# Sums of squares halved on VectorE, paired compression matmuls, weight splits moved to GpSimd at four joints, and first loads in halves

## The reference, cut to what matters

```python
def first_block(x, ...):
    h = x
    for layer in range(2):
        if layer == 1:
            shared = nsa_shared_kv(h, kv_norm, kv_w, ...)   # k and v of three branches; one is compressed by an MLP
        normed = rms_norm(h, mix_norm_pre[layer])
        mixed = retention_mixer(normed, ...) if layer == 0 else nsa_mixer(normed, ..., shared)
        h = h + rms_norm(mixed, mix_norm_post[layer])
        normed = rms_norm(h, ffn_norm_pre[layer])
        h = h + rms_norm(swiglu_ffn(normed, ...), ffn_norm_post[layer])
    return h

def second_block(x, ...):
    h = modulate(rmsnorm(x, norm1_g), sh1, sc1)
    u_a, v_a, q, k, v, gates = split(h @ w_in)              # k and v also for a context of 256 tokens
    merged = g_a * (chunk_gmlp(u_a, v_a) @ w_proj_a) + g_b * (window_gqa(q, k, v, ...) @ w_proj_b)
    x = x + g1 * (merged @ w_out)
    h2 = modulate(rmsnorm(x, norm2_g), sh2, sc2)
    return rmsnorm(x + g2 * expert_choice_ffn(h2, ...), final_g)   # 16 experts, 32 tokens each
```

## Time and profile before

| | |
|---|---|
| median of three runs | 2094.96 us (2092.45 to 2096.02) |
| time of the profiled execution | 2095.24 us |
| span of its trace | 2093.4 us |
| mean granted TensorE clock | 0.903 |
| busy: TensorE, VectorE, ScalarE, GpSimd | 1661.2, 709.5, 579.1, 113.8 us |
| read from HBM | 594.71 MB |

### The profile page before, as it was taken

The page is one execution under the profiler, slowest core; times in us unless marked ns, Lnnn a source line. Parts: engine busy times, 40 slices in busy tenths (PEclk is TensorE's granted clock), DMA queues, the critical chain, the costliest instruction groups (busy, mean ns, idle before and its releaser), DMA issues.

```text
span 2093.4 us, 27147 instructions
## 1 busy us (share of the span) xinstructions
PE 1661.2 (79%) x11764; PEld 1155.0 (55%) x11764; DVE 709.5 (34%) x1020; ACT 579.1 (28%) x959; POOL 113.8 (5%) x127
## 2 busy tenths in 40 slices
PE   7999999999889999999996765565556565555665
PEld 7899999998469999897796311111111111111111
DVE  5456655563656755657655100000000000000001
ACT  4455444443665344436652100000000000000000
POOL 1001000000310300002300000000000000000000
PEclk9999999999999999999998978878887878888777
DMA  9545685557694655263265799999999999999995
GB/s 305 185 141 178 120 247 185 186 172 217 246 316 149 207 185 183 81 202 103 100 262 201 304 427 430 426 429 427 428 428 427 429 426 429 427 428 428 429 427 214
DMA packets 156380, 603.54 MB, mean 288 GB/s; under 512 B 6550, under 2 KB 109127, under 8 KB 128471
## 3 DMA queue, kind: packets, MB, share of 16 engines
q1 hardware_dynamic: 147712, 587.23, 71.8%
q10 hardware_dynamic: 7704, 11.23, 1.8%
q0 software_dynamic: 864, 3.61, 1.5%
HBM read 594.71 MB, written 4.19 MB: 286 GB/s over the span
## 4 chain that ended last, share of the span: by engine, by line
PE 52%; DMA 41%; DVE 4%; ACT 2%; issue 1%; POOL 0%; DVEq 0%; ACTq 0%
PE ps L663 19%; DMA dense_tables<-in_w_exp_gate 13%; DMA dense_tables<-in_w_exp_up 13%; DMA dense_tables<-in_w_exp_down 13%; PE ps L732 11%; PE ps L717 3%; PE ps L1230 2%; PE ps L1089 2%; PE ps L685 2%; PE ps L640 1%; DVE split_operands L572 1%; PE ps L1251 1%; PE ps L1122 1%; PE ps L1112 1%; PE ps L897 1%
## 5 line engine op out<-in xcount | busy, mean ns | idle before, releaser
L572 DVE TENSOR_TENSOR split_operands<-dense_ring,split_operands 128x1024 fp32r<-128x1024 f32 x288 | 349.9, 1257 | 272.7 <-ACT split_operands L564 272.4
L663 PE MATMUL ps<-split_operands 128*128 128x256 f32 x3456 | 426.0, 284 | 15.9 <-DVE split_operands L572 13.2
L663 PEld LDWEIGHTS ps<-split_operands 128*128 128x128 f32 x3456 | 419.7, 193 | 17.4 <-issue 14.0
L564 ACT ACTIVATE split_operands<-dense_ring 128x1024 fp32r<-128x1024 f32 x288 | 288.6, 1050 | 324.4 <-PE ps L663 159.5
L2226 DVE TENSOR_TENSOR arena<-arena,ps 128x512 f32<-128x512 f32 x16 | 11.0, 688 | 861.2 <-PE ps L1230 861.2
L1230 PE MATMUL ps<-dense_ring,arena 128*32 128x512 f32 x624 | 99.8, 771 | 80.1 <-DMA dense_ring<-in_w_exp_gate 41.4
L1230 PE MATMUL ps<-late_expert_slots,arena 128*32 128x512 f32 x592 | 105.0, 845 | 71.8 <-DMA late_expert_slots<-in_w_exp_up 36.0
L732 PE MATMUL ps<-split_operands 128*128 128x256 f32 x1248 | 151.6, 283 | 2.4 <-DVE split_operands L582 2.1
L732 PEld LDWEIGHTS ps<-split_operands 128*128 128x128 f32 x1248 | 150.2, 192 | 4.4 <-DVE split_operands L582 2.5
L1230 PE MATMUL ps<-arena 128*32 128x512 f32 x624 | 93.6, 726 | 59.7 <-DMA arena<-in_w_exp_gate 33.9
L732 PE MATMUL ps<-hidden_split,split_operands 128*128 128x256 f32 x960 | 118.6, 283 | 0.8 <-DVE split_operands L572 0.8
(11 more groups left out here) (297 smaller groups left out, 1739.8 us busy)
## 6 DMA issues: line engine op xcount, KB each, us to landing
dense_ring<-in_ffn_w_in SPq DMA_DIRECT2D x44, 1024.0 KB, 5.1
arena<-in_w_exp_gate SPq DMA_DIRECT2D x20, 2048.0 KB, 46.8
dense_ring<-in_w_exp_up SPq DMA_DIRECT2D x20, 2048.0 KB, 46.5
late_expert_slots<-in_w_exp_down SPq DMA_DIRECT2D x20, 2048.0 KB, 46.7
dense_ring<-in_w_exp_gate SPq DMA_DIRECT2D x19, 2048.0 KB, 46.2
arena<-in_w_exp_up SPq DMA_DIRECT2D x19, 2048.0 KB, 45.9
late_expert_slots<-in_w_exp_up SPq DMA_DIRECT2D x19, 2048.0 KB, 45.6
arena<-in_w_exp_down SPq DMA_DIRECT2D x19, 2048.0 KB, 45.5
```

What stands on the lines that cost most here:

```text
L564: act.activation(w_hi[:, n % 2, c], ring[U % RING][:, c], ACT.Copy).then_inc(hi_ready, 1)
L572: dve.tensor_tensor(w_lo[:, n % 2, c], ring[U % RING][:, c], w_hi[:, n % 2, c], ALU.subtract).then_inc(lo_ready, 1)
L663: mm = pe.matmul(ps[:, bank, b * T:b * T + T], left, right, start=k == 0 and i == 0, stop=k == 7 and i == 2)
```

## The change

What it does, by parts:

- **Squares.** `add_squares` on VectorE adds chunks of squares before TensorE sums them. The four norms ahead of a block (`N_PRE0`, `N_PREF0`, `N_PRE1`, `N_PREF1`) then need 2 ones matmuls instead of 8, the four in the joints 4, and retention's heads 2 instead of 4. In `pair_products` the norm now stands behind all products.
- **Joints.** ScalarE runs a tiny Sqrt before the squares, and `roots` before the split of U+1. VectorE no longer splits U+1: GpSimd does.
- **Compression.** k and v are multiplied in turn, in columns 0 to 59 and 64 to 123 of the array; the four weight units are loaded in that order.
- **K and V.** `U_K` and `U_V` leave `WHOLE`: the tokens' keys and values come from split units. The context's stay unsplit.
- **Start.** x is passed in with 4 KB rows by half, and x and the first unit are loaded in halves, in turn; splits and products of the first unit go by halves.

```diff
-WHOLE = set(range(U_W1, U_NQ)) | set(range(U_ADA, U_NO)) | {U_IN2 + 4, U_IN2 + 5}
+WHOLE = set(range(U_W1, U_NQ)) | set(range(U_ADA, U_NO))
+ADDED = {N_PRE0: (0,), N_POST0: (0, 3), N_PREF0: (0,), N_POSTF0: (0, 3), N_PRE1: (0,), N_POST1: (0, 3),
+         N_PREF1: (0,), N_POSTF1: (0, 3)}
 # SyncE
-            sp.dma_start(h[:], a["xT"].rearrange("(k p) t -> p k t", p=P)).then_inc(x_in, 16)
+            for half in range(2):
+                k = slice(4 * half, 4 * half + 4)
+                sp.dma_start(h[:, k, :], a["x_rows"].rearrange("p (k t) -> p k t", k=DC)[:, k, :]).then_inc(x_in[half], 16)
+                sp.dma_start(slot8(U_RET)[:, k, :], first[:, k, :]).then_inc((half_landed, landed[0])[half], 16)
 # TensorE
-                for q in range(4):
-                    pe.wait_ge(sq_ready, 4 * n + q + 1)
+                for q in ADDED.get(n, range(4)):
+                    if n in ADDED and q == 0:
+                        pe.wait_ge(sq_added, 2 * n + 2)
+                    else:
+                        pe.wait_ge(sq_ready, 4 * n + q + 1)
                     for c in (2 * q, 2 * q + 1):
...
                 mm.then_inc(used, 1)
-                between()
                 for k in range(4, 8):
                     mm = chunk(1, k)
                 mm.then_inc(used, 1)
+                norm(n)
...
-                pe.wait_ge(osq, hd + 1)
-                for e in range(4):
-                    mm = pe.matmul(ps[:, 4, 0:T], ones[:], sq[:, e, :], start=e == 0, stop=e == 3)
+                pe.wait_ge(osq_added, hd + 1)
+                for e in range(2):
+                    mm = pe.matmul(ps[:, 4, 0:T], ones[:], sq[:, e, :], start=e == 0, stop=e == 1)
...
+                    for w in range(2):
+                        for kind in range(2):
+                            take(U_W1 + 2 * w + kind)
+                        for c in range(8):
+                            for kind in range(2):
+                                mm = pe.matmul(ps[64 * kind:64 * kind + 60, kind, 0:T], blocks[:, kind, 8 * w + c, :],
+                                               slot8(U_W1 + 2 * w + kind)[:, c, :], start=w == 0 and c == 0,
+                                               stop=w == 1 and c == 7)
...
-            keys(xn, 7).then_inc(used, 1)
-            values(xn, 4).then_inc(used, 1)
+            col_T(U_K, 7)
+            col_tok(U_V, 4)
 # ScalarE, post()
                 split_hi(act, U)
+                act.activation(table_of[:], ones[:, 0:1], ACT.Sqrt)
...
+                roots(n)
                 split_hi(act, U + 1)
-                roots(n)
 # ScalarE, compression
+                rows = slice(64 * kind, 64 * kind + 60)
+                taken(act, U_W1 + 2 + kind)
+                act.activation(cmp_hid[rows, 0:T], ps[rows, kind, 0:T], ACT.Silu).then_inc(c_act, 1)
                 split_hi(act, U_NQ + kind)
 # VectorE
+            def add_squares(n):
+                steps = ((4, 4, 4), (2, 2, 4)) if len(ADDED[n]) == 1 else ((2, 2, 2), (2, 4, 3))
+                for i, (chunks, other, squared) in enumerate(steps):
+                    dve.wait_ge(sq_ready, 4 * n + squared)
+                    if i:
+                        dve.wait_ge(sq_added, 2 * n + i)
+                    dve.tensor_tensor(sq[:, 0:chunks, :], sq[:, 0:chunks, :], sq[:, other:other + chunks, :],
+                                      ALU.add).then_inc(sq_added, 1)
...
                 split_lo(dve, U)
-                split_lo(dve, U + 1)
+                add_squares(n)
                 inverse(n)
...
+                add_squares(n)
+                dve.wait_ge(lo_ready, 2 * SPLIT_NO[gate_unit(f, 0) + 1] + 2)
                 split_lo(dve, gate_unit(f, 1))
                 inverse(n)
...
-            for U in (U_IN2 + 2, U_IN2 + 3, U_UA):
+            dve.wait_ge(lo_ready, 2 * SPLIT_NO[U_IN2 + 1] + 2)
+            for U in (U_IN2 + 2, U_IN2 + 3, U_K, U_V):
                 split_lo(dve, U)
 # GpSimd, each in its place in the queue
+            split_lo(pool, U_F0 + 1)
             pool.wait_ge(brow_ev, 1)
             pool.dma_start(bias_dram, ...)
+            split_lo(pool, U_KV + 1)
...
+            split_lo(pool, U_F1 + 1)
             pool.wait_ge(gains_set, 1)
...
+            split_lo(pool, U_IN2 + 1)
```

More of the change, by code:

```diff
@@ L473, in load_expert @@
                 sp.dma_start(dst, src).then_inc(e_landed[g % ERING], 16)
-            for u in range(24):
+            for u in range(1, 24):
                 if 8 <= u < 16:
@@ L673, in col_tok, with pair_products @@
                 col_products(U, bank, lambda b, w, x: (x[:, b * P:b * P + P], w), 0, x0)
-            def pair_products(U, banks, place, x0, between):
+            def pair_products(U, banks, place, x0, n):
                 def chunk(v, k):
@@ L756, in _ @@
             pe.wait_ge(ones_set, 1)
-            for u in range(2):
-                col_products(U_RET + u, 5 + 2 * u, lambda b, w, x: (w[:, b::2], x), x0=X_RET if u == 0 else None)
-                if u == 0:
-                    norm(N_PRE0)
+            hi, lo = parts_of(U_RET)
+            for k in range(8):
+                if k % 4 == 0:
+                    pe.wait_ge(lo_ready, k // 4 + 1)
+                pe.wait_ge(xlo_ready, k + 1)
+                for b in range(2):
+                    for i, (w, x) in enumerate(((hi, x_hi), (hi, x_lo), (lo, x_hi))):
+                        mm = pe.matmul(ps[:, 5, b * T:b * T + T], w[:, k, b::2], x[:, k, :],
+                                       start=k == 0 and i == 0 and b == 0, stop=k == 7 and i == 2,
+                                       skip_group_check=True)
+            mm.then_inc(used, 1)
+            norm(N_PRE0)
+            col_products(U_RET + 1, 7, lambda b, w, x: (w[:, b::2], x))
             pe.wait_ge(first_in, FIRST_IN)
@@ L874, in _ @@
             bias_table(1)
-            pair_products(U_KV, (1, 3), by_feature, X_KV, lambda: norm(N_PRE1))
+            pair_products(U_KV, (1, 3), by_feature, X_KV, N_PRE1)
             for u in range(2, 6):
```

77 lines of the change are left out of this document (43 added, 34 removed).

## The result

The changed kernel took 2082.19 us in the median of 7 runs (2078.64 to 2089.28). The kernel before, on the same chip, took 2094.96 (2092.45 to 2097.47). The ratio is 0.9945, 95% interval [0.9927, 0.9963], so 12.8 us are gained (8 to 15 by the interval). 2081 had been forecast, and a range of 2067 to 2089.

A forecast was written before the change was run, and what follows sets the result against it. The DMA-bound expert stream starts when the dense stage ends, so dense savings reach the end. 5.6 - 4.6 - 2.0 + 7.8 + 3.8 + 2.3 + 1.2 = 14.1 off 2095.24 gives 2081, range 2067 to 2089.

The forecast's parts named there:

- Start: Up to the third unit: loading in halves brings the first product 3.0 us earlier, shorter sums save 2.6; gain 5.6.
- Norms behind pairs: Three norms behind pair products: 2 ones matmuls instead of 8 save 2.6 us each, 7.8 in all.
- The cover of 0.5: Behind the pair norms: 0.5 us spare before TensorE waits for a split; failing costs up to 1 at each of two places.
- Joints: Four joints: root 1.7 us earlier, but GpSimd's splits delay residual adds by 2.9; 1.2 lost each, 4.6 in all.
- Clock: First pair products behind the joints: longer TensorE idling lowers the granted clock; 2.0 us lost.
- Compression: Key and value products side by side take 7.5 us instead of 13.95, then TensorE waits 2.6 for a split; gain 3.8.
- K and V: Tokens' keys and values: split units take 5.75 us each instead of 6.91; gain 2.3.
- retention: Retention heads: 2 of 4 sum matmuls go, but VectorE's scale is late next; 0.4 us each for three heads, 1.2.
- Rival 1: At the joints GpSimd doesn't hold up VectorE's chunk loop: 27.5 us off, 2068; chance 0.20.
- Rival 2: Compression's two kinds don't run side by side and halves bring nothing at the start: 2090.5 us; chance 0.14, either alone included.
- Rival 3: At the joints GpSimd's halves come so late that TensorE waits for U+1: slower, 2111 us; chance 0.04.
- Rival 4: The stream of experts is pinned otherwise, so the dense gain is lost: no change, 2095 us; chance 0.05.

The follow-up runs named there:

- both edits together: Changed kernel with GpSimd's second split halves held until the fourth low slice, and ScalarE splitting the first two attention units ahead of both Silu; 2074.50 us.
- quarters: Changed kernel with each of GpSimd's four splits in four instructions of 128x512 instead of two of 128x1024; 2081.67 us, ratio 0.9934.

## Why the profiled execution was faster than the median

The repeat of the changed kernel agrees with the first profile to 0.2 us at every stage up to the middle of the attention stage (481.91 and 481.94 at the next unit behind the compression, 540.62 and 540.67 there). Then it falls behind by 3.3 within ten microseconds. TensorE's timeline, first the first profile of the changed kernel:

```profile
540.62 0.65 PE L997 MATMUL ps<-arena 128*64 128x256 f32 x4 [2.58 <-ACT arena L1525]
...
545.51 1.07 PE L793 MATMUL ps<-dense_ring,cond_silu 128*32 128x512 f32 x8
```

and the repeat, with one stretch of its clock:

```profile
540.67 0.65 PE L997 MATMUL ps<-arena 128*64 128x256 f32 x4 [2.58 <-ACT arena L1525]
...
548.77 1.07 PE L793 MATMUL ps<-dense_ring,cond_silu 128*32 128x512 f32 x8
```
```profile
543.00:545.00 2.00, 2.00 (x12) 1.42 (x8) 1.87 (x8) 0.74 (x6) 0.65 (x2) 0.50 0.00 0
```

The same wait of 2.58 us stands ahead of the same products in both. In one execution the clock stays at 1.00 behind it, and in the other it falls to 0.50 for some 6 us, and 3.3 us are lost. The fall also shows in the profile of the kernel before, and in nine of the thirteen profiles of this study's kernels, with or without the change. Three of the four profiled executions without it are the fastest of their kernel, and none of the nine with it is. In this sense the fall is chance. With the fall in both, the attention stage of the table is 142.5 us in the repeat and 141.4 in the kernel before; the 1.1 was not followed up.

The repeat loses more: 1.4 in the pair of `U_F1`, where 96 products take 14.5 us instead of 13.1, and some 1.2 behind 940 us. So its first expert product starts 6.0 us later than in the first profile (1156.58 against 1150.56). But its span is only 3.1 longer, since its expert stage takes 923.1 us and not 925.9. In the fourteen profiles that stage took 923.1 to 923.6 us five times, 924.9 once, and 925.9 to 926.9 eight times. What decides this was not found; it is not the start, for it took 926.8 in the kernel before (start 1166.6) and 926.4 with both edits together (start 1144.0), but 923.4 where the norms behind pairs were undone (start 1165.4). Falls of the clock and this step are each as large as most terms of the forecast, which is why the terms are read from stages. How the 4 us between 16.9 (spans) and 12.8 (medians) divide among them is not shown.

## Why the prediction was right

The forecast, 2081, was 1.2 us off, by terms that mostly measured as they were worked out. The sum is closer than its terms: a wait of 1.4 that it lacked, and 0.7 less at the start and in retention, are made up for by joints, pairs and compression that came out 0.5 to 0.7 better each. That part is luck.

- **Start**: 5.2 against 5.6, split into halves 2.85 (3.0) and sums 2.36 (2.6).
- **Norms behind pairs**: 7.3 for a forecast of 7.8. The cover of 0.5 that I had called the thinnest held: there is no wait behind the norms at line 677 or 746 that was not there before.
- **Joints**: each loses 0.9 to 1.0, forecast 1.2. Both sides were somewhat too large. The root comes 1.4 earlier, not 1.7, since the sum waits 0.41 for VectorE's second add. The adds lose 0.63 and 1.76, 2.4 together, not 0.9 and 2.0.
- **Clock**: forecast 2.0 lost. In the timeline 96 products at full clock take 11.7 us. In the changed kernel they take 13.3, 14.2 and 13.1 at the three pairs, so 5.5 is lost. Before, the first 72 took 10.8, 10.8 and 8.9, where 8.8 is full clock: 4.1. That is 1.4 more in the first profile, and 2.6 more in the repeat (13.2, 14.1 and 14.5).
- **Compression**: 7.12 us and a wait of 2.64, forecast 7.5 and 2.6. What the forecast lacked is the 1.4 ahead of it. The blocks made of the shifted keys are late next: the keys are issued 10.4 us earlier and TensorE arrives 9.4 earlier, but the blocks start only 7.4 earlier. In the profile before, the blocks were ready just 0.6 ahead of the products; that could be read, and I did not ask for it. It would have warned of the wait, though not of the slower transfer.
- **K and V** 2.3 (2.3), **retention** 0.87 (1.2).

Taking from the table only what the change did, the terms give 5.2 + 0.9 - 3.9 + 6.4 - 1.4 + 4.3 + 2.3 = 13.8, for 14.1 forecast and 12.8 measured. **Rival 1** fell by the adds of 1.04 and 2.17. **Rival 2** fell by 7.12 and by 9.74. **Rival 3** is excluded, since GpSimd's half takes 2.4 us and not 7.4. **Rival 4** fell: the expert stage took 925.9 us instead of 926.8 while its start moved by 16.

## What to carry to other kernels

Work moved to GpSimd is not free because GpSimd is idle: one of its instructions with two SBUF inputs held up each VectorE add with two SBUF inputs until it ended. Place it where VectorE is not on the path (here the second half behind the fourth slice, worth 7.0 us at four joints by the trace and some 10 by the times), or cut it so small that a turn is short. And when TensorE's work between two points shrinks, look at the transfers that run beside it: here they shrank less, and a wait of 1.3 to 1.6 us appeared that no sum of engine times held. Last, compare stages at the same clock: one removed wait of 2.64 us looks like 0.5 or like 3.1, by the run that it is set against. The version with the later second half, 2074.67 us, beats both kernels.

## What the runs showed that was not expected

- GpSimd's turns: a residual add of 0.41 us took 1.04 to 2.52 beside GpSimd, by how much of the running GpSimd instruction was left: 1.04 behind a half that ended 0.8 later, 2.17 behind one that ended 1.9 later, 2.52 behind one that had just begun. Each ended 0.28 behind it, and with quarters queued too (1.19 and 1.09) it waited for one instruction only.
- Two groups of products with 60 columns each took 7.12 us side by side in alternation, and 13.22 in turn (1.7 of that an estimate of the clock's part, from 8.81 less 7.12).
- Behind a pause of up to 1.56 us ahead of the compression the clock was at 1.00 in all its products, in eight profiles; behind pauses of 1.95 to 2.44 it was at 0.50 in some of them, in five, and in the four of these that alternate the products took 8.81 us instead of 7.12. But behind 2.58 in the attention stage it fell in some executions and not in others.
- The expert stage took 923 us in some profiles and 926 in others, whatever its start.
